# Split products for the mixer's input projection and the first block's out projection, with two expert weight slots loaded later

## The reference

```
# first block
h = rms_norm(x); proj = h @ w_in
conv_out = conformer_conv(proj[conv]);  attn_out = diff_attention(q, k, v)
merged = gate0 * (conv_out @ w_conv_out) + gate1 * (attn_out @ w_attn_out)
x = x + merged @ w_out                      # the out projection, 1024 x 1024
x = x + hierarchical_moe(rms_norm(x))       # 32 experts, 2 per token, all weights read
# second block
xn = rms_norm_2(x) ; proj = xn @ w_in_2     # the mixer's input projection
ya = short_conv_mixer(pa); yb = dilated_mixer(pb)
yc = forgetting_mixer(pc); yd = pool_mixer(pd)
x = x + concat(ya, yb, yc, yd) @ w_out_2
x = x + memory_cross_attention(rms_norm_2(x), rms_norm_2(mem))
x = x + conv_ffn(rms_norm_2(x)); return rms_norm_2(x)
```

## Time and profile before

| | us |
|---|---|
| median of 3 runs | 1088.74 |
| lowest and highest | 1088.71, 1091.20 |
| profiled execution | 1092.08 |
| its span | 1089.9 |
| TensorE busy | 954.7 (88%) |
| VectorE busy | 457.0 (42%) |
| ScalarE busy | 314.1 (29%) |
| HBM read | 298.90 MB |

### The profile page before, as it was taken

How to read it: one execution, slowest core, us unless ns; L and a number is a source line. 1 busy time by engine, 2 the same in 40 slices (tenths; PEclk the granted TensorE clock), 3 DMA queues, 4 the chain that set the end, 5 groups by cost and what they waited for, 6 DMA issues and landing times.

```text
span 1089.9 us, 13781 instructions
## 1 busy us (share of the span) xinstructions
PE 954.7 (88%) x5834; PEld 684.3 (63%) x5834; DVE 457.0 (42%) x774; ACT 314.1 (29%) x514; POOL 1.3 (0%) x5
## 2 busy tenths in 40 slices
PE   7999999999978686677676776899999999999998
PEld 6968888895424232222222131378889999999986
DVE  5769876151101001010101010153974567888842
ACT  5421451021101010000000010232563736566632
POOL 0000000000000000000000000000000000000000
PEclk9999999989989888878788796999999999999999
DMA  8693413579999999999999999992035243656451
GB/s 311 230 366 138 155 39 155 193 270 367 425 424 420 425 426 426 422 428 422 430 423 430 422 428 425 404 328 77 2 109 201 78 155 118 193 161 220 161 193 38
DMA packets 76889, 300.75 MB, mean 276 GB/s; under 512 B 3745, under 2 KB 30498, under 8 KB 60194
## 3 DMA queue, kind: packets, MB, share of 16 engines
q1 hardware_dynamic: 75520, 298.89, 69.8%
q10 hardware_dynamic: 1314, 1.07, 0.4%
HBM read 298.90 MB, written 1.05 MB: 275 GB/s over the span
## 4 chain that ended last, share of the span: by engine, by line
PE 69%; DMA 27%; ACT 1%; DVE 1%; SPq 1%; issue 1%; DVEq 0%; ACTq 0%; PEldq 0%
PE bank L646 17%; PE bank L1263 10%; DMA ring<-in_w_down_e_dram 8%; DMA ring<-in_w_gate_e_dram 8%; DMA ring<-in_w_up_e_dram 8%; PE bank L952 7%; PE bank L1281 6%; PE bank L1149 3%; PE bank L1164 3%; PE bank L733 3%; PE bank L673 3%; PE bank L656 3%; PE bank L1005 3%; DMA qvpr<-in_w_down_e_dram 2%; PE bank L977 2%; PE bank L666 1%
## 5 line engine op out<-in xcount | busy, mean ns | idle before, releaser
L952 PE MATMUL bank<-ring,big 128*32 128x512 f32 x768 | 157.8, 691 | 61.8 <-DMA ring<-in_w_up_e_dram 36.7
L952 PEld LDWEIGHTS bank<-ring,big 128*32 128x32 f32 x768 | 35.8, 125 | 177.9 <-issue 93.2
L344 DVE TENSOR_TENSOR ring_parts<-ring,ring_parts 128x2048 fp32r<-128x2048 f32 (+1 forms) x54 | 118.8, 2249 | 36.1 <-ACT ring_parts L336 35.8
L336 ACT ACTIVATE ring_parts<-ring 128x2048 fp32r<-128x2048 f32 (+1 forms) x54 | 98.5, 1874 | 48.8 <-DMA ring<-in_w_up_dram 26.1
L646 PE MATMUL bank<-hs,ring 128*128 128x256 f32 x448 | 98.0, 379 | 0.0
L646 PEld LDWEIGHTS bank<-hs,ring 128*128 128x128 f32 x448 | 85.0, 190 | 13.1 <-issue 1.7
L952 PE MATMUL bank<-qvpr,big 128*32 128x512 f32 x112 | 68.7, 771 | 22.9 <-DMA qvpr<-in_w_up_e_dram 11.5
L1263 PE MATMUL bank<-mrg_parts,ring_parts 128*128 128x256 f32 x640 | 82.3, 281 | 0.0
L1945 DVE TENSOR_TENSOR xT<-bank,xT 128x512 f32<-128x512 f32 x32 | 22.1, 692 | 139.8 <-PE bank L991 139.8
L1263 PEld LDWEIGHTS bank<-mrg_parts,ring_parts 128*128 128x128 f32 x640 | 78.5, 189 | 0.0
L952 PE MATMUL bank<-hs,big 128*32 128x512 f32 x128 | 70.6, 707 | 1.4 <-DMA hs<-in_w_up_e_dram 0.8
(11 more groups left out here) (331 smaller groups left out, 1464.8 us busy)
## 6 DMA issues: line engine op xcount, KB each, us to landing
ring<-in_w_gate_e_dram SPq DMA_DIRECT2D x24, 2048.0 KB, 20.0
ring<-in_w_up_e_dram SPq DMA_DIRECT2D x24, 2048.0 KB, 28.8
ring<-in_w_down_e_dram SPq DMA_DIRECT2D x20, 2048.0 KB, 21.3
ring<-in_w_in_dram SPq DMA_DIRECT2D x13, 2048.0 KB, 13.5
ring<-in_w_up_dram SPq DMA_DIRECT2D x22, 1024.0 KB, 6.7
qvpr<-in_w_down_e_dram SPq DMA_DIRECT2D x5, 2048.0 KB, 25.6
ring<-in_w_down_dram SPq DMA_DIRECT2D x5, 2048.0 KB, 7.9
ring<-in_w_out_dram SPq DMA_DIRECT2D x4, 2048.0 KB, 8.5
```

The lines of the kernel that those rows point to most:

```text
L336: signal(act.activation(pairs[stage][u % 3][0][:, part], raws[stage][u % 3][:, part], ACT.Copy), stage + "_hi")
L344: signal(eng.tensor_tensor(lo[:, part], raws[stage][u % 3][:, part], hi[:, part].bitcast(F32), ALU.subtract), name)
L952: mm = pe.matmul(bank[part][CAP * j:CAP * j + CAP, :], xeT[:, c, CAP * j:CAP * j + CAP], w[j][c], start=(c == 0), stop=(c == DC - 1))
```

## The change

- The out projection of the first block (`wo`) takes the split form. ScalarE rounds its two units into slots 0 and 5 (`round_out`), VectorE makes the remainders (`rest_of_out`), and the merged activations are rounded by ScalarE, chunk by chunk, with the remainder by VectorE. The first unit's four outputs are made chunk by chunk side by side, the second's one after the other.
- Slots 0 and 5 are thereby in use until the out projection is through, and SP loads units 0 and 6 of the first expert group in the order 1, (late keys), 0, 2, 6, 3.
- `co` 4 and 5 stand behind `o1` on TensorE, and VectorE's products with them behind `mem_sum`.
- Units 1 to 4 of the mixer (pieces 2, 3, 4 and 0 of the weights) take the split form (`split_post`, `round_post`, `rest_of_post`), with `mix_hi` and `mix_lo` for the normed input. Unit 0 stays plain.
- On VectorE the order in the mixer is new: norm, rest of unit 1, products of `pa` and `qb` with the root, forget gates, `mix_lo`, rest of unit 2, the arguments from `posb`, rotation, `c_rows`, rest of unit 3, maxima, four reciprocals, rest of unit 4, four reciprocals, pool, rest of `ff` 0. The rest of `ff` 1 comes after the next stage's input. On ScalarE Sin, Exp and Ln stand behind the moves of `kb` and `vb`; `ff` 0 is rounded after the scaled shares, and `ff` 1 behind the `aT` moves.
- The multiplicities are in the mask, as 8 log(multiplicity), under the scale of 1/8; the product with them and the new sum are gone, and the division of all eight score tiles is done by ScalarE, as a scale.
- The raw units of `ff` go to slots 4, 5 and 0, with rounded parts in 2, 1 and 3; the first three wait for `kc 1`, `pd 1` and `pa 3`. The forget heads' scores lie in `qko`, the pool's tiles in `big`.

```diff
-    add("dil_mask", np.where(mult > 0, 0.0, -BIG))
-    add("dil_mult", mult)
+    add("dil_mask", np.where(mult > 0, 8.0 * np.log(np.maximum(mult, 1.0)), -BIG))
+    add("gain_space", np.zeros((P, 512)))
...
-    split_at = {"in": ..., "ff": [tuple((POST_AT + j + i) % RING for i in range(2)) for j in (-1, 1, 3)]}
+    split_at = {"in": ..., "ff": ((2, 4), (1, 5), (3, 0))}
...
-        FF_FREE = [("qb", 1), ("kc", 1), ("pa", 3)] + ...
+        FF_FREE = [("kc", 1), ("pd", 1), ("pa", 3)] + ...
...
+        OUT_HI = (0, 5)
+        mix_hi, mix_lo = parts["sq"], parts["hT"]
+        POST_HI = {1: 1, 2: 2, 3: 1, 4: 3}
...
 # SP, first expert group
-                load_unit(0, 0)
-                load_unit(0, 6)
                 load_unit(0, 1)
                 sp.wait_ge(S["merged"], 8)
                 sp.dma_start(late_w, w_xkv[:, :, 768:1024]).then_inc(S["keys_in"], 16)
-                for u in (2, 3):
+                for u in (0, 2, 6, 3):
                     load_unit(0, u)
...
 # TensorE, out projection
             for u in range(2):
-                w = u512(pre_unit(pe, 2 + u))
-                for m in range(4):
-                    linear(("wo", 4 * u + m), w, m, mrg, ready="merged" if (u, m) == (0, 0) else None)
+                w_hi, w_lo = u512(ring_r[OUT_HI[u]]), u512(ring_r[2 + u])
+                for ms in ((range(4),) if u == 0 else ((m,) for m in range(4))):
+                    for which, (w, x) in enumerate(((w_hi, mrg_hi), (w_lo, mrg_hi), (w_hi, mrg_lo))):
+                        for k in range(8):
...
+                freed.append(used[OUT_HI[u]])
                 freed.append(used[2 + u])
...
 # TensorE, mixer
+            def split_post(j, *groups):
+                s = (POST_AT + j) % RING
+                w_hi, w_lo = u512(ring_r[POST_HI[j]]), u512(ring_r[s])
+                for g, outs in enumerate(groups):
+                    for which, (w, x) in enumerate(((w_hi, mix_hi), (w_lo, mix_hi), (w_hi, mix_lo))):
+                        for i, (use, at) in enumerate(outs):
+                            b = begin(pe, use) if which == 0 else bank[PLACE[use][0]]
+                            for k in range(8):
...
+            split_post(1, [(("kb", 0), 0), (("kb", 1), P)], [(("vb", 0), T)], [(("vb", 1), T)])
...
+            split_post(2, *([((("qc", "kc")[m // 2], m % 2), P * m)] for m in range(4)))
...
+            split_post(3, [(("vc", 0), 0)], [(("vc", 1), 0)], [(("pd", 0), T)], [(("pd", 1), T + P)])
+            split_post(4, *([(("pa", m), P * m)] for m in range(4)))
...
 # ScalarE, mixer
             root(("nmix", 0))
+            round_post(1)
+            for c in range(DC):
+                act.wait_ge(S["normed"], NORMS["nmix"] + c + 1)
+                signal(act.activation(mix_hi[:, c * T:c * T + T], hT[:, c * T:c * T + T], ACT.Copy), "mix_hi")
+            arrive(act, ("qb", 1))
+            round_post(2)
+            for m in range(2):
+                move(("kb", m), big[:, (8 + m) * T:(9 + m) * T], T)
+            for t in range(TT):
+                move(("vb", t), vtok[:, 512 * t:512 * t + 256], 256)
             act.wait_ge(S["ang"], 2)
             signal(act.activation(pad[:, 0:512], pad[:, 0:512], ACT.Sin), "trig")
...
+            round_post(3)
...
+            round_post(4)
...
+                    ins = act.activation(e, e, ACT.Copy, scale=st[:, s8 + 6 + t:s8 + 7 + t])
...
             for name, base in (("b", 0), ("c", FORGET)):
                 for h in range(4):
                     move(("aT" + name, h), item(base + 512 * h), 512)
+            round_weights(1)
...
 # VectorE, mixer
             normalise(("nmix", 0), "g_mix", xT, hT)
+            rest_of_post(1)
+            # pa, qb by the root; f; mix_lo, moved here or new
+            rest_of_post(2)
             b = arrive(dve, ("posb", 0))
```

More of the change, by code:

```diff
@@ L221, in two_blocks_kernel @@
         landed_post = [sem(f"weights_landed_post{i}") for i in range(RING)]
-        used_post = [sem(f"weights_used_post{i}") for i in range(RING)]
         raw_landed = {stage: [sem(f"raw_landed_{stage}{i}") for i in range(3)] for stage in ("in", "ff")}
         names = """x_hi x_lo up_tap in_hi in_lo h1_hi h1_lo ff_hi ff_lo pair_used h_hi h_lo up_val act_hi act_lo ident_in const_in par_in x_in pos_in wf_in mem_in out_done dve_step act_step zeroed squares normed lam_in
-                   lam_exp qk_ready s_max s_exp a_ready conved conv_dev conv_z conv_sig mem_sum x_gain mix_sum conv_out attn_out merged
+                   lam_exp qk_ready s_max s_exp a_ready conved conv_dev conv_z conv_sig mem_sum out_hi out_lo mrg_hi mrg_lo x_gain mix_sum mix_hi mix_lo post_hi post_lo s_inv conv_out attn_out merged
                    logits pair_gap g_exp e_exp member rounds picked pick_step hid_step swt_full rows_full swt rows gate_sig
@@ L298, in two_blocks_kernel @@
         split = {"in": w_in_units, "ff": ffn}
[L299 removed]
+        split_at = {"in": ((5, 0), (1, 2), (3, 4)), "ff": ((2, 4), (1, 5), (3, 0))}
         raws = {n: [ring[lo] for _, lo in at] for n, at in split_at.items()}
@@ L792, in _ @@
             w_conv = w
-            for m in range(6):
+            for m in range(4):
                 linear(("co", m), w_conv, m, big[:, 16 * T:20 * T], 4)
@@ L807, in _ @@
                                     kt == 0, kt == 1) for kt in range(2)])
+            for m in range(4, 6):
+                linear(("co", m), w_conv, m, big[:, 16 * T:20 * T], 4)
             b = begin(pe, ("nmem", 0))
@@ L1411, in _, with round_out @@
             root(("on", 1))
+            def round_out(u):
+                for i in range(2):
+                    act.wait_ge(landed[2 + u], 16)
+                    part = slice(UW // 2 * i, UW // 2 * (i + 1))
+                    signal(act.activation(ring_r[OUT_HI[u]][:, part], ring[2 + u][:, part], ACT.Copy), "out_hi")
+            arrive(act, ("co", 7))
+            round_out(0)
             for m in range(3):
                 move(("kx", m), att[:, (8 + m) * T:(9 + m) * T], T)
+            arrive(act, ("gt", 15))
+            round_out(1)
+            for m in range(DC):
+                act.wait_ge(S["merged"], m + 1)
+                signal(act.activation(mrg_hi[:, m * T:m * T + T], mrg[:, m * T:m * T + T], ACT.Copy), "mrg_hi")
             square_residual("wo", sq)
@@ L1519, in _ @@
                 move(("pd", m), pool_x[:, m, 16:16 + T], T)
+            for i in range(4):
+                scaled_shares(12 + i, FORGET + 512 * i)
+            round_weights(0)
             for m in range(4):
@@ L1821, in _, with rest_of_out @@
             gated_conv(range(6, 8))
+            def rest_of_out(u):
+                for i in range(2):
+                    dve.wait_ge(S["out_hi"], 2 * u + i + 1)
+                    part = slice(UW // 2 * i, UW // 2 * (i + 1))
+                    signal(dve.tensor_tensor(ring_r[2 + u][:, part], ring[2 + u][:, part],
+                                             ring_r[OUT_HI[u]][:, part].bitcast(F32), ALU.subtract), "out_lo")
+            rest_of_out(0)
             for m in range(8):
@@ L1830, in _ @@
                 signal(dve.tensor_tensor(y, y, g, ALU.add), "merged")
+            for i in range(2):
+                dve.wait_ge(S["mrg_hi"], 4 * i + 4)
+                part = slice(1024 * i, 1024 * i + 1024)
+                signal(dve.tensor_tensor(mrg_lo[:, part], mrg[:, part], mrg_hi[:, part].bitcast(F32), ALU.subtract), "mrg_lo")
+            rest_of_out(1)
             def residual(use, n=8):
@@ L2041, in _ @@
             signal(dve.tensor_tensor(z, z, pool_x[:, :, 16:], ALU.subtract), "z_pool")
[L2042 to L2045, removed]
+            rest_of_both("ff", 0)
             for m in range(6):
@@ L2069, in _ @@
             rest_of_input(0, parts["hT"], hT, parts["big"])
-            rest_of_both("ff", 2)
+            for u in (1, 2):
+                rest_of_both("ff", u)
             residual("w2")
```

164 lines of the change are left out of this document (97 added, 67 removed).

## The result

The changed kernel takes 1079.95 us (median of 6 runs, 1079.34 to 1082.01). Its runs stand to those of the kernel before as 0.9902, 95% interval 0.9889 to 0.9916, which is 10.7 us of 1091. Forecast were 9.8 us, 1079 us and so a ratio of 0.991. Runs of the kernel before had a median of 1088.74 at first and of 1091.78 over 19 runs beside the experiments (1089.03 to 1093.21), so ratios are safer here than differences of medians. The profiled execution took 1080.13 us, its span is 1078.3: 11.6 less than before, more than the runs show.

A forecast was written before the change was run, and what follows sets the result against it. TensorE was taken to hold 69% of the chain and DMA 27%. First block 5.65 plus mixer 4.15 gave 9.8 us off the 1088.74 us median, so 1079 us, range 1075 to 1084.

The forecast's parts named there:

- Price of a product: Out projection and mixer: one 128x256 output takes 2.88 us as three fp32r products, against 3.45 us as f32.
- First block: Up to the out projection's end: nmem 1.1 us earlier plus 4.6 us from split products, 5.65 us unrounded.
- The wait of 1.1 for head 3: First block: head 3's transposes must wait for VectorE's last difference, so TensorE loses some 1.1 us.
- The stream starts as much earlier: Expert weight loads: the displaced loads fill free DMA time, so the full 5.6 us of lead is kept.
- the backlog of 2 us: DMA at 241.4 us: queue left by the later loads when the next 3 MB can be asked for; 2 us.
- Mixer: From the experts' end to w2: 9.2 us saved on split products, less new waits, leaves 4.15 us.
- the wait for `posb`: Mixer, ahead of vb 0: TensorE waits for posb's bank, which VectorE frees behind the rest of unit 2; 3.4 us.
- Rival 1: Mixer: the wait at vb 0 drops TensorE's clock to 1.2 GHz; 1081.5 us; chance 18%.
- The hole of 2.28 us: First block, until mem_sum: TensorE idle 2.28 us with the clock still 1.00; by it the mixer's wait would cost no clock.
- (2): Mixer: VectorE is quicker to posb, or TensorE comes later, and no wait arises; 1075.5 us; chance 10%.
- (3): Mixer: ScalarE and VectorE bind throughout, further waits eat all 9.2 us; 1083.1 us; chance 12%.
- (4): Expert loads: both displaced loads stand wholly before the stream, 10.0 us more; 1094.6 us; full 4%, in part 4%.

The follow-up runs named there:

- first block only: Kernel before with only the first block's part: split out projection, conv outputs 4 and 5 moved, slots 0 and 5 loaded later; ratio to before 0.9936.
- shares on VectorE: Changed kernel with the shares of all eight score tiles on VectorE again, multiplicities as a product with a new sum; 1089.19 us.
- positions early: Changed kernel with one VectorE instruction, the first product on posb, moved ahead of the rest of unit 2; 1075.15 us.
- kept busy: Changed kernel with seven useless matmuls on TensorE where it waits for the positions' bank; 1078.75 us.
- three moves: Changed kernel with the first posb product early, only conv output 5 behind o1, and the next stage's unit 1 rounded behind the input's rounding; 1074.38 us.
- mixer only: Kernel before with only the mixer's part of the change; ratio to before 0.9965.
- slots later only: Kernel before with only the loads of units 0 and 6 of the first experts moved behind the out projection's halves; ratio to before 1.0004.

## Why the prediction was right, step by step

- **Price of a product.** 2.88 us an output forecast. The out projection took 22.72 us instead of 23.04, the mixer's groups 11.50 for four and 17.28 for six. Right.
- **First block.** 5.65 us forecast at the end of the out projection, 5.99 measured: 1.09 at its head (167.21 to 166.12), 4.9 in the projection. The wait of 1.1 for head 3 came as forecast (1.14), no wait came inside the projection. The projection's gain was forecast 0.3 short, since its matmuls stand 0.118 us apart and not 0.12.
- **The stream starts as much earlier.** All of the lead was to be kept. Here the step was off in both directions. The later loads cost 0.5 to 1.2 us, which I had taken as nothing: I had set the backlog of 2 us against an estimated start of an idle DMA of before that is as long, and no run shows that second term. And the lead at the first expert product was 8.7 and not 6.0, for the clock in the router's stretch, which the forecast did not mention, though the 0.93 of the earlier trace rows points at it. It fell in the profile of before, and did not in that of after. The last expert load started 7.4 us earlier (668.87, now 661.52), where 5 to 6 was forecast.
- **That clock is partly chance, and perhaps partly the change.** With the same code up to the experts, the clock fell in first block only and in shares on VectorE, and did not in the changed kernel, its second profile, positions early and kept busy; in three moves it fell for a shorter stretch. With the plain projection it fell in three of three. A full fall costs 2.7 us ahead of the first expert product: the router stretch takes 27.53 or 27.54 in all five profiles that have one, and 24.83 to 24.85 in the four that have none. Ten profiles don't tell whether the split form makes the fall rarer. The runs hint at it: those of first block only lie in two groups, 1083.5 to 1084.4 (four) and 1087.1 to 1087.2 (two), and the profiled one, with the fall, is in the upper; seven of eight runs of the changed kernel lie within 1.4 us of each other and the eighth 1.3 above them, while 32 of 40 runs of the kernel before lie above 1090, 1 to 5 us over its lowest. That these groups are this fall is not shown, since only the profiled executions have a clock by stretch. Of the 11.6 us between the spans 2.2 to 2.7 are this fall, and it is a likely reason why the spans differ by more than the runs (10.7).
- **Mixer.** 4.15 us forecast, 3.8 measured (102.71 to 98.92). Inside: the wait for `posb` 3.4 forecast, 3.11 measured, on the instruction and the bank that were named. The wait ahead of w2 grew by 0.34 to 1.17 and not by 1.1; ScalarE's four moves there took 1.28 in all and started 0.4 earlier than I had it; kc's wait of 0.3 and mix_lo's of 0.25 came as some 0.1 each. The waits were thus forecast 1.4 us too large. Against that stand the clock, with 1.5 us, and the slower restart of vb behind the hole, with 0.26 (6.02 for 5.76).
- **Rival 1 came true too.** I had given it 18% and priced 1.7 to 3.4. In both profiles of the changed kernel and in mixer only, the clock fell behind the wait of 3.1 us, and vb took 7.27 to 7.52 for the 6.02 of shares on VectorE, where it did not fall behind the same wait: 1.25 to 1.5 us, below what I had priced. So the forecast left out a clock term that came, and its mixer number held because another error cancelled it.
- **The whole number was in part luck.** In the two profiles, 9.8 became 11.5 at w2: 0.3 more from the first block, 2.7 more from the router's clock, 1.0 less from the expert stretch, 0.4 less from the mixer. The mechanisms forecast for the products, the bank of `posb` and the start of the stream are right; that the sum came within a microsecond of the runs' 10.7 rests also on two clock terms, one for and one against, that the forecast did not have.
- **The rows on the clock.** I had read the earlier trace rows as a fall after 3.85 us of idle. The window before those shown is this:

```profile
311.00:314.00 3.00, 1.04 (x2) 0.14 (x2) 0.47 (x1) 0.00 (x0) 0.00 (x0) 1.00 1.01 431
```

The wait of 3.85 began at 313.93 (317.78 less 3.85), and 0.55 over 314 to 317 means that the clock fell in the first 0.3 us of that window. So it fell when the second wait had hardly begun, behind the 2.17 us of idle and 1.04 of matmuls before it, and the row never said that a wait must last 3.85. The hole of 2.28 us, by which I left the clock out, did not carry over to 3.1.
- **The rule on gaps.** The Trainium skill, "TensorE: Matmul & The Clock Gate", in the row on gaps between matmul bursts of its section "Why this matters for your kernels", has an idle TensorE go back to half rate. For the wait of 3.1 us the trace agrees in three profiles of four, and in the fourth it does not.
- **Rivals 2 to 4.** VectorE was not quicker (2). The waits did not eat all of the mixer's gain (3), though shares on VectorE shows that mechanism when the relief is gone. The displaced loads do not stand in front of the stream (4): slots later only is at 1.0004.

## What to carry to other kernels

When banks are inherited in a fixed order, an instruction that frees a bank is part of the critical path however little it computes: before putting new work in front of it, ask whose bank it holds. Price a wait of TensorE like this one of 3.1 us with the slow stretch behind it, here 1.5 us in three profiles of four, and remember that useless matmuls in the wait bring back at most the latter. When a profile of before and one of after differ in a stretch that the change doesn't touch, take more profiles before giving it to the change.

## What was not expected of the hardware

- The granted clock fell in the router's stretch in some executions and not in others of kernels with the same code up to there, with TensorE busy throughout; the fall stands in or behind the router's products, which are matmuls of 36 columns each (229.21 to 233.20 in the kernel before, whose clock is 0.89 in 230 to 233 us and 0.50 behind). It costs 2.7 us where it happens, of which 2.2 to 2.7 reach the end of the experts' weights: from the out projection's end to the experts' last products the same code takes 476.95 and 477.30 with the fall, and 474.64 to 474.75 without. What decides it stays open.
- Two kernels with the same wait of 3.1 us at the same place differ in whether the clock falls behind it (vb 7.50 and 6.02). What decides it was not found.
